# Reordering the opening, the block ends, one gate unit and the last matmuls of a one-core hybrid decoder layer

## What is computed

```python
shift1, scale1, gate1, shift2, scale2, gate2 = split(silu(c) @ w_ada + b_ada, 6)   # adaLN
h = rmsnorm(x, norm1_g) * (1 + scale1) + shift1
gq, gk, gv, gr, glr, aq, ak, av, ga, gb = split(h @ w_in)
y_a = (rmsnorm(gla(q, k, v, log_sigmoid(glr @ wg2 + bg) / 16)) * silu(gr)) @ w_branch_a
y_b = combine(dilated_attention(aq, ak, av) for 3 groups) @ w_branch_b
x = x + gate1 * ((sigmoid(ga) * y_a + sigmoid(gb) * y_b) @ w_out)
h2 = rmsnorm(x, norm2_g) * (1 + scale2) + shift2
a, b = split(h2 @ w_up); x = x + gate2 * ((silu(causal_conv3(a)) * b) @ w_down)
y = rmsnorm(x, normf_g)            # plus new GLA state, windows and conv state
```

## Time and profile before

| what | us |
|---|---|
| median of 3 runs | 1250.01 |
| the profiled execution, its own time | 1249.03 |
| its span in the trace | 1247.3 |
| PE matmul busy | 1187.5 (95%) |
| DVE busy | 617.7 (50%) |
| ACT busy | 447.0 (36%) |
| POOL busy | 107.6 (9%) |

### The profile page before, as it was taken

The page is one execution under the profiler, slowest core; times in us unless marked ns, Lnnn a source line. Parts: engine busy times, 40 slices in busy tenths (PEclk is TensorE's granted clock), DMA queues, the critical chain, the costliest instruction groups (busy, mean ns, idle before and its releaser), DMA issues. The chain is left out here.

```text
span 1247.3 us, 23079 instructions
## 1 busy us (share of the span) xinstructions
PE 1187.5 (95%) x9681; PEld 1117.0 (90%) x9681; DVE 617.7 (50%) x999; ACT 447.0 (36%) x652; POOL 107.6 (9%) x189
## 2 busy tenths in 40 slices
PE   5899999999989999999997899999999999999997
PEld 3878998888889998989886799989999999999997
DVE  4432134645415544266586365548655655633333
ACT  3264333454434342343343353224333333222222
POOL 0000010111011001100310011000110110010000
PEclk9899999999989999999998999988999999999999
DMA  9664459773364224423437478613888887256661
GB/s 304 207 211 140 136 171 347 248 216 120 104 190 137 94 94 136 136 87 110 158 125 222 175 232 288 203 35 102 282 291 259 264 285 236 80 191 222 224 227 69
DMA packets 166016, 229.39 MB, mean 184 GB/s; under 512 B 7644, under 2 KB 148342, under 8 KB 164636
## 3 DMA queue, kind: packets, MB, share of 16 engines
q1 hardware_dynamic: 148720, 123.72, 32.5%
q10 hardware_dynamic: 1684, 54.56, 12.0%
q0 software_dynamic: 15536, 50.01, 11.8%
HBM read 204.58 MB, written 81.87 MB: 230 GB/s over the span
## 5 line engine op out<-in xcount | busy, mean ns | idle before, releaser
L378 PE MATMUL ps<-actH,whi 128*128 128x260 f32 x2064 | 433.9, 292 | 12.1 <-PEq L1245 4.8
L378 PE MATMUL ps<-actH,wlo 128*128 128x260 f32 x2064 | 418.2, 284 | 0.0
L378 PE MATMUL ps<-actL,whi 128*128 128x260 f32 x2064 | 417.6, 284 | 0.0
L378 PEld LDWEIGHTS ps<-actH,whi 128*128 128x128 f32 x2064 | 320.4, 191 | 32.4 <-issue 26.6
L378 PEld LDWEIGHTS ps<-actL,whi 128*128 128x128 f32 x2064 | 321.0, 190 | 0.0
L378 PEld LDWEIGHTS ps<-actH,wlo 128*128 128x128 f32 x2064 | 320.8, 190 | 0.0
L362 DVE TENSOR_TENSOR wlo<-wraw,whi 128x2048 fp32r<-128x2048 f32 (+2 forms) x95 | 141.3, 1499 | 157.1 <-ACT whi L349 156.8
L349 ACT ACTIVATE whi<-wraw 128x2048 fp32r<-128x2048 f32 (+2 forms) x95 | 119.3, 1275 | 133.0 <-PE ps L378 90.0
L433 ACT ACTIVATE arena<-ps 128x520 f32<-128x520 f32 x74 | 44.5, 601 | 208.1 <-PE ps L378 193.1
L378 PE MATMUL ps<-gH,whi 128*128 128x260 f32 x352 | 71.1, 283 | 0.0
L378 PE MATMUL ps<-gH,wlo 128*128 128x260 f32 x352 | 70.8, 282 | 0.0
(11 more groups left out here) (339 smaller groups left out, 1365.8 us busy)
## 6 DMA issues: line engine op xcount, KB each, us to landing
wraw<-in_w_in SPq DMA_DIRECT2D x38, 1024.0 KB, 5.4
out_win_s<-in_cache_win ACTq DMA_DIRECT2D x16, 2046.0 KB
wraw<-in_w_up SPq DMA_DIRECT2D x44, 512.0 KB, 5.8
out_win_s<-in_cache_win ACTq DMA_DIRECT2D x8, 2044.0 KB
wraw<-in_w_ada SPq DMA_DIRECT2D x14, 1024.0 KB, 6.2
arena<-in_w_ada SPq DMA_DIRECT2D x10, 1024.0 KB, 12.7
raw_gates<-arena SPq DMA_DIRECT2D x24, 260.0 KB, 6.9
arena<-raw_gates POOLq DMA_DIRECT2D x24, 260.0 KB, 4.2
```

What stands on the lines that cost most here:

```text
L378: last = pe.matmul(ps[:, 2 * (n % 2) + a, 0:HT], wt, X[:, k0 + j, a * HT:a * HT + HT], start=begin and j == 0 and wt is hi and X is H, sto ...
```

## The change

Five things, all of them orders and places, no arithmetic:

1. **Opening.** The transposes of `v2row` and `csrow` and their copies move ahead of x; `root_dve` and tile 0's fold come before `ada_dve` of tile 1, and the root is spread before tile 1's fold; the low part of the first weight unit is made in four quarters, each ahead of `low(2j)`, where it was one instruction behind `low(0)`; in PE's loop each pair is now tile 2j, first output tile of `dense(k)`, fold of 2j, tile 2j+1, second output tile, fold of 2j+1, `dense(k+1)`.
2. **Block ends.** Five `nc.Block()` get `no_gpsimd_drain=True` (one of them is the loop over groups 0 and 1, so all six bodies).
3. **One `ga` unit** moves from group 0 (9 units, now 8) to group 2 (4 units, now 5).
4. **`wo` units:** `square_dve` of the tile before goes ahead of the wait for the tile's passes.
5. **FFN block:** PE's last conv tail waits for one copy less and the wait for all 22 gate tiles becomes 11 and 22; at the end the sums are split and go to bank 3, and y_sample is stored by ACT's queue.

```diff
-    add("aq1 aq1 ga ak1 ga ak1 av1 ga av1", "att0")
+    add("aq1 aq1 ga ak1 ga ak1 av1 av1", "att0")
     add("aq2 aq2 ak2 ak2 av2 av2", "att1")
-    add("gb gb gb gb", "att2")
+    add("gb gb ga gb gb", "att2")
...
@@ head_dve
+            dve.wait_ge(s("prep_T"), 3)
+            dve.tensor_copy(vec[:, NV1:NV1 + NV2], ps[:, 5, 0:NV2])
+            dve.tensor_copy(stT[:, :, :], ps[:, 5, P:P + KF * 16].rearrange("p (k b) -> p k b", b=16)).then_inc(s("vec_ready"), 1)
             for k in range(KD):
                 dve.wait_ge(s("x_T"), k + 1)
...
             mean_dve(dve, ss, tok1)
-            ada_dve(dve, 1, ada1)
             root_dve(dve, 0, tok1)
             ada_turn_dve(dve, 0)
+            ada_dve(dve, 1, ada1)
             ada_turn_dve(dve, 1)
...
                 normed(j)
                 if j < 3:
                     ada_dve(dve, 2 * j + 2, ada1)
+                split_lo(dve, 0, j, 4)
                 low(2 * j)
-                if j == 0:
-                    split_lo(dve, 0)
                 if j < 3:
+                    ada_turn_dve(dve, 2 * j + 2)
                     ada_dve(dve, 2 * j + 3, ada1)
-                    ada_turn_dve(dve, 2 * j + 2)
                 low(2 * j + 1)
...
@@ head_pe
             ada_pe(pe, 0)
...
+            ada_turn_pe(pe, 0, ada1)
             ada_pe(pe, 1)
-            ada_turn_pe(pe, 0, ada1)
-            ada_turn_pe(pe, 1, ada1)
             pe.wait_ge(s("operand_ready"), 2)
             spread_root_pe(pe, 0, tok1)
+            ada_turn_pe(pe, 1, ada1)
+            pe.wait_ge(s("x_evac"), KD)
             for j in range(1, 4):
+                k = 2 * j - 2
                 ada_pe(pe, 2 * j)
+                dense(k, 0)
+                ada_turn_pe(pe, 2 * j, ada1)
                 ada_pe(pe, 2 * j + 1)
-                ada_turn_pe(pe, 2 * j, ada1)
...
-                dense(2 * j - 2)
+                dense(k, 1)
                 ada_turn_pe(pe, 2 * j + 1, ada1)
-                dense(2 * j - 1)
+                for m in range(2):
+                    dense(k + 1, m)
...
-        with nc.Block() as block:
+        with nc.Block(no_gpsimd_drain=True) as block:
...
+                        square_dve(dve, 1, 2 * j + m - 1, n2)
                         dve.wait_ge(pass_done, passes[n])
                         residual_dve(dve, n, 2 * j + m, 2 * KD)
-                        square_dve(dve, 1, 2 * j + m - 1, n2)
...
-                pe.wait_ge(s("tail_tok"), KF - 1)
+                pe.wait_ge(s("tail_tok"), KF - 2)
                 pe.transpose(ps[0:NS + 2, 7, 0:P], abuf[:, 1, TP:T + 2], ident).then_inc(s("tail_T"), 1)
-                pe.wait_ge(s("g_lo"), KF)
...
                         pe.wait_ge(lo_ready, vd0 + 2 * m + half + 1 + 4 * i)
+                        if m == 0 and first:
+                            pe.wait_ge(s("g_lo"), KF // 2 * (half + 1))
...
-                sp.wait_ge(s("y_tok"), 5)
-                sp.wait_ge(s("y_tok_dve"), 5)
-                sp.dma_start(o["y_sample"], ysst).then_inc(s("y_out"), 16)
...
+                act.wait_ge(s("y_tok"), 5)
+                act.wait_ge(s("y_tok_dve"), 5)
+                act.dma_start(o["y_sample"], ysst).then_inc(s("y_out"), 16)
```

More of the change, by code:

```diff
@@ L555, in ada_turn_dve, with sums_pe @@
                               ALU.add).then_inc(ada_read, 1)
-        def sums_pe(pe, bank, part, first):
+        def sums_pe(pe, bank, col, part, first):
             for n in range(5):
                 m = P if n < 4 else NS
-                last = pe.matmul(ps[0:m, bank, n:n + 1], part[:, P * n:P * n + m], ones[:, 0:1], start=first and n == 0,
+                last = pe.matmul(ps[0:m, bank, col + n:col + n + 1], part[:, P * n:P * n + m], ones[:, 0:1], start=first and n == 0,
                                  stop=not first and n == 4, skip_group_check=True)
@@ L802, in head_pe @@
             pe.transpose(ps[:, 6, 0:NV1], v1row, ident[0:NV1, 0:NV1]).then_inc(s("prep_T"), 1)
+            pe.wait_ge(s("late_in"), E0)
+            pe.transpose(ps[:, 5, 0:NV2], v2row, ident[0:NV2, 0:NV2])
+            for k in range(KF):
+                last = pe.transpose(ps[:, 5, P + 16 * k:P + 16 * k + 16], csrow[:, P * k:P * k + P], ident[0:16, 0:16])
+            last.then_inc(s("prep_T"), 1)
             pe.wait_ge(s("x_in"), 80)
@@ L809, in head_pe @@
                 last.then_inc(s("x_T"), 1)
+            pe.wait_ge(s("vec_ready"), 2)
             for k in range(KD):
@@ L813, in head_pe, with dense @@
             pe.wait_ge(s("operand_ready"), 1)
[L814 to L816 removed]
+            def dense(k, m):
                 x = U[U_HEAD]
[L818 to L822, removed]
[L824 to L830 removed]
+                if m == 0:
+                    pe.wait_ge(s("h_split"), k + 1)
+                last = three_pass(pe, m, 0, [x["block"](k, m)], actH, actL, k0=k, begin=k == 0, end=k == KD - 1)
+                if k == KD - 1:
+                    last.then_inc(pass_done, 1)
+            ada_pe(pe, 0)
+            ada_turn_pe(pe, 0, ada1)
             ada_pe(pe, 1)
[L832 to L833 removed]
             pe.wait_ge(s("operand_ready"), 2)
             spread_root_pe(pe, 0, tok1)
+            ada_turn_pe(pe, 1, ada1)
+            pe.wait_ge(s("x_evac"), KD)
             for j in range(1, 4):
+                k = 2 * j - 2
                 ada_pe(pe, 2 * j)
+                dense(k, 0)
+                ada_turn_pe(pe, 2 * j, ada1)
                 ada_pe(pe, 2 * j + 1)
[L839 to L847 removed]
+                dense(k, 1)
+                ada_turn_pe(pe, 2 * j + 1, ada1)
+                for m in range(2):
+                    dense(k + 1, m)
+            for k in (KD - 2, KD - 1):
+                for m in range(2):
+                    dense(k, m)
         gk, gq, gv = at(0, 4, T), at(2080, 4, T), at(4160, KD, T)
@@ L2556, in _ @@
                     turn(n, range(KD - 1))
-                pe.wait_ge(s("x_new"), 2 * KD)
                 pe.wait_ge(s("sq_added"), 2 * (KD - 2))
+                sums_pe(pe, 3, YS, n3["t"], True)
                 pe.wait_ge(s("sq_ready"), 2 * KD)
-                last_sq = n3["sq"][:, (KD - 1) % 2, :]
-                for n in range(5):
-                    m = P if n < 4 else NS
-                    for x, part in enumerate((n3["t"], last_sq)):
-                        last = pe.matmul(ps[0:m, 1, YS + n:YS + n + 1], part[:, P * n:P * n + m], ones[:, 0:1],
-                                         start=x == 0, stop=x == 1)
-                last.then_inc(s("sq_summed"), 1)
+                sums_pe(pe, 3, YS, n3["sq"][:, (KD - 1) % 2, :], False).then_inc(s("sq_summed"), 1)
                 pe.wait_ge(s("gained"), KD)
                 for n in range(3):
+                    if n == 2:
+                        pe.wait_ge(s("ms_ready"), 3)
                     turn(n, [KD - 1]).then_inc(s("y_T"), 1)
-                turn(4, range(4))
-                pe.wait_ge(s("ms_ready"), 3)
-                turn(4, range(4, KD)).then_inc(s("y_T"), 1)
+                turn(4, range(KD)).then_inc(s("y_T"), 1)
                 for half in range(2):
```

12 lines of the change are left out of this document (4 added, 8 removed).

## The result

The changed kernel takes 1243.24 us (median of 8 runs, 1240.88 to 1247.10); the kernel before takes 1250.19 beside it (8 runs). The ratio is 0.9943, 95% interval 0.9928 to 0.9957, so 7.1 us less (5.4 to 9.0). Forecast were 14.8 less, 1235.2, with a range of 1228 to 1243; the measured median lies 0.2 above it. The sign was right, the size was half. The profiled execution took 1242.61 us, its span is 1240.9 (before: 1249.03 and 1247.3).

What follows compares the result with a forecast made beforehand. PE was taken to bound the kernel, so only its waits and half-clock stretches counted. From 1250.01 us, -6.3 - 9.0 - 2.6 - 1.0 - 0.2 + 4.3 = -14.8 gave 1235.2, range 1228.0 to 1243.0.

Steps and rivals of the forecast that it cites:

- block ends: At the first block's end POOL's drain goes, PE's wait falls from 4.78 to 1.10 us at full speed: -6.3.
- ga unit: Attention group 2: a fifth unit spreads steps, the late spill's 6.2 us wait and its half speed go: -9.0.
- boundary, wo, end: Up to down projection wait goes, -2.6; wait before the output projection's sums goes, -1.0; y_sample stored earlier, -0.2.
- opening: First block: earlier root gains 0.8, but low-part quarters delay PE in the tile pairs and the clock falls: +4.3.
- So 9.2 becomes 2.2: PE's waits inside group 2: 1.3 us remain at the join and 0.9 of the small waits, 7.0 saved.
- Group 0 at 0: Group 0 with 32 steps in 32 places costs nothing, dense matmuls between steps covering them; bounds -0.5 and +3.
- +1.2 a pair: Opening's tile pairs: PE idles 1.8 instead of 0.64 us for DVE's low part behind a weight quarter.
- Rival A: The opening gains, full speed from the first pair on making it -1.5: 1229.4 in all; chance 0.14.
- The rule on queues: DMA engines alternate queues packet by packet; read as an equal share for the group 2 spill, so no late spill.
- B: Rival: low clock lasts through the opening, which then costs +10: 1240.9 in all; chance 0.09.
- C: Rival: the spill in group 2 is still late, the ga term is only -3: 1241.2 in all; chance 0.09.
- E: Rival: the block flag does not take POOL's drain away, 6.3 less gained: 1241.5; chance 0.06.

Runs made afterwards that it cites:

- second half: Only the quarters of the weight's low part ahead of even tiles and dense work between paired tiles, added to the kernel before: 1261.03 us, ratio 1.0065.
- first half: Only the vector transpositions ahead of x and the root first, added to the kernel before: 1248.88 us, ratio 0.9973.
- the version with the spill wait moved: Changed kernel with the old opening, its wait for the last spills moved from SP at group 2's end to ACT in the next block: 1235.39 us, ratio 0.9853.

## Why the prediction was wrong, step by step

| term | forecast | alone on the chip | 95% |
|---|---|---|---|
| block ends | -6.3 | -5.3 | -7.3 to -3.3 |
| ga unit | -9.0 | -4.0 | -5.8 to -2.4 |
| boundary, wo, end | -3.8 | -4.5 | -6.6 to -2.5 |
| opening | +4.3 | +4.9 | +2.9 to +6.9 |
| sum | -14.8 | -8.9 | change: -7.1 |

**The ga unit is the step that failed**, 5 of the 7.7 us by which the forecast missed. Of the rest the other terms make 0.9 together, and 1.8 is what the four parts alone sum to beyond the change, within its interval and not explained. Its main claim was right: with the fifth unit the spill precedes the bulk load, and the 6.2 us wait and its half speed went. The mis-sized parts, by the trace of the unit alone:
- "So 9.2 becomes 2.2": group 2's waits became 4.9, 2.7 more. The chain at the join was right (0.9; I had 1.3, though its terms, 1 + 1.05 + 0.6 - 1.45, give 1.2). The small waits were not: 0.9 was to remain of them, and it was 4.0. I counted steps per place, not what shares DVE with them: a weight quarter of 0.68 us stands ahead of a step's chain (the wait of 1.7) and another comes late itself (1.3). I had allowed for such a quarter only in the join.
- I took the 3.9 us at the end of group 2 as staying. It became 5.7. The weight load ahead of the last spills now leaves 0.4 us behind the beginning of PE's drain, where it left 2.3 us before it, and SP waits 4.0 us for the last spill instead of 2.2. The same SP order, weight before spill, that I read in the middle of the phase stands at its end too, and I didn't follow it there. This wait was also the largest thing left to gain: moving it gave 3.5 to 4.6 us in three pairs of kernels.
- Group 0 at 0, "since most steps there already stand in neighbouring places": its own wait of 1.1 went (-1.5 in all) and one of 1.1 came at its end, where the last step now stands in the last place. By chance the cost of 0 was nearly right; the places at its end, which I hadn't looked at, were not.

**The block ends** were right, in mechanism (no drain of POOL, 1.16 us, full speed) and within the interval in size. **The boundary** and **the wo units** were right: the 2.59 and 0.97 us went. **The end** was not: -0.2 was forecast because "the same 20 sum matmuls follow the same transposes", and it measured +0.2 by the marks (14.6 to 14.8), since the last transposes now run at half speed. What in the new order brings that about, no run separates.

**The opening** was right in total and partly for the wrong reason. The pairs' waits of 1.9 us were forecast as 1.8. "+1.2 a pair" and the clock's +2.0 make +5.1 for the second half; on the new first half it measured 8.3 (4.9 + 3.4) in time, with some 2.6 to either side, and 5.2 by the marks: the first matmul of the unit behind tile 8 starts 57.1 us behind x with both halves (mean of 57.0 and 57.2) and 51.9 with the first alone (mean of 51.7, 52.5 and 51.4). So the waits and the marks bear it out, and its size isn't settled better than 5 to 8. The first half was forecast at -0.8 for its waits. It gave -3.4 (and -1.9 on top of the version with the spill wait moved), and I had given the clock no gain there: a stretch at half speed of 13.7 or 10.2 us becomes 10.2 or 6.8. Rival A spoke of this gap and this clock, and it fell because the quarters then take the gain back.

**The rule on queues.** One sign of the forecast did not come: "ACT's copy behind a spill starts without a DMA wait" holds for the copy at the join, but the trace of after has ACT waiting 13.76 us for a later spill, until 690.09. PE doesn't wait for that copy. DMA rows of 676 to 691 us (packets, MB, share; then KB, us to landing):

```profile
q0 software_dynamic: 144, 2.13, 38.1%
q1 hardware_dynamic: 1328, 1.58, 32.3%
...
arena<-gla_out POOLq DMA_DIRECT2D x1, 2080.0 KB, 11.0
wraw<-in_w_ada SPq DMA_DIRECT2D x1, 1024.0 KB, 13.4
raw_gates<-arena SPq DMA_DIRECT2D x2, 260.0 KB, 13.7
```

The spill lands last, and 2 MB on POOL's queue (q0) land sooner than 1 MB on SP's (q1). Cut to 679 to 681 us:

```profile
q0 software_dynamic: 46, 0.77, 90.8%
q1 hardware_dynamic: 45, 0.05, 7.0%
```

The two queues got as many packets, but q0's are of 14.8 KB on average and q1's of 1.2 KB (2.13 MB / 144 and 1.58 MB / 1328), so in these 2 us q0 moved 15 times the bytes and had 13 times the engines' time; and within SP's queue the spill stands behind 1 MB. The Trainium skill (DMA: Bandwidth & Descriptors, Queues, rings and completion order) says that an engine takes turns between queues packet by packet. The rows fit that rule; they don't fit the equal share that I had read out of it.

**The range.** It reached up to 1243.0, just past the times of B, C and E (1240.9 to 1241.5), each of which supposed one miss, and it left out what lay beyond. The ga term then missed at two places, by 2.7 and 1.8 us, neither of which was among the rivals: C had about the right size (-3 for the ga term, measured -4.0) for the wrong reason, since the spill it spoke of did land in time.

## What to carry to other kernels

When work is moved into a phase to cover its waits, list what ends last at each of the phase's ends as well: a shorter phase meets the same last transfer earlier. Count what each place holds on the busiest helper engine, not only how many steps. Time one large change in its parts: here one of four parts lost 5 us, half of that part gained 3, and the sum hid both.

## What the runs showed of the hardware

The time of a whole execution varied by 7.5 us (1248.63 to 1256.10 for the kernel before, 17 runs in one set) with the same instructions. Over the 79 runs of the kernel before in the four sets, all 17 with a mean granted clock of 0.977 or less took 1253.9 us or more, and of the other 62 only 2 did. The traces of the variants show where such differences lie: in the opening the first stretch at half clock is 10.2 or 13.7 us, behind L2527 none or 3.4, around the end of group 2 none to 6.8. What such a stretch costs can be read behind L2527: from the second adaLN's fold to the last dense pair the two traces with 3.4 us at half clock there take 392.0 and 392.1 us, and the seven with the same code and without it 390.1 to 390.2, so it costs 1.9. One profiled execution is therefore a sample for a clock term, and I had used it as the value.

A weight quarter of 0.6 us in DVE's path, in each pair, cost 4.6 us in time (some 2.3 to either side), of which one pair of traces shows no more than 1.5 in PE's waits; the rest isn't accounted for. Behind the first block's end, too, a wait was worth more than its length (3.6 us of wait, 5.3 in time); there the windows show the half speed that goes with it.
